# PEER of a two-block network on one core: one-hot in pairs of tokens, a ring of 66 results, and another place for the first reads of the routing weights

## The chip, the cores and the metric

The kernel runs on one core of one Trainium2 chip. The metric is device time in microseconds (us). The engines of a core work in parallel and meet through semaphores: TensorE (PE, with PEld for its weight loads), VectorE (DVE), ScalarE (ACT), GpSimd (POOL) and SyncE (SP), which here only issues transfers. Sixteen DMA engines carry the transfers of all queues.

## What is computed

The reference is a small network over 256 tokens of width 1024, in fp32: a first block (two layers, each SwiGLU, convolution and attention, SwiGLU) and a second block (two layers, each a mixer and a PEER feed-forward). The change touches PEER alone, which runs twice:

```python
def peer_ffn(h, w_query, sub_keys, expert_u, expert_v):      # h: 256 x 1024
    q = (ht @ w_query).reshape(T, 8, 2, 128)
    scores = einsum('thpd,hpkd->thpk', q, sub_keys)          # 128 keys a half
    s_top, i_top = lax.top_k(scores, 16)
    cand = s_top[:, :, 0, :, None] + s_top[:, :, 1, None, :]
    cand_idx = i_top[:, :, 0, :, None] * 128 + i_top[:, :, 1, None, :]
    best, pos = lax.top_k(cand, 16)                          # 16 of 256, 8 heads
    gates = softmax(best)
    ...                                                      # for each token t, k = 1..128
    a = gelu(einsum('tkd,td->tk', expert_u[idx], xb)) * g
    out = einsum('tk,tkd->td', a, expert_v[idx])
```

There are 16384 experts (128 first indices i times 128 second indices j), and a token uses 128 of them.

## The kernel before

**Dense PEER.** The kernel doesn't gather experts. It multiplies all tokens with all experts and sets the unused ones to zero by a dense table of routing weights, 16384 by 256 tokens. A layer of PEER has these stages on the tensor engine:

1. Queries, key scores and, between them, the first up-weights. The vector engine finds the top 16 meanwhile.
2. **The build of the table** (function `g_products`). Tokens come in 16 groups g of 16. For each token, TensorE multiplies two one-hot matrices of fp16: `Ah` (128 slots by 128 values of i, times the weight, in two parts z) and `Bh` (128 slots by 128 values of j). This gives a 128 x 128 table of the token in PSUM, with 32 matmuls a group. Between the groups TensorE takes 1 or 2 up-weight units in turn (the list `DUE`), 24 in all.
3. **The up-only pairs.** The pairs of up-weight units from NTOP + NBUILD = 29 up to NPAIRS - 1 follow.
4. **The v stage.** For n = 0 to 63: two units of down-weights (`peer_v`), and while there are any left, the pair n + NPAIRS of up-weights.

**Units.** A unit is a 128 x 1024 piece of fp32 weights; a chunk of 1 MB holds two, and SyncE loads it into one of NRAW = 3 raw buffers. ScalarE makes the high part w_hi (L1069), then VectorE the low part w_lo (L1502; for some units of the first stage GpSimd, L2079), then TensorE uses both (L583 to L585 for up-weights, L588 to L590 for down-weights). There are NPAIR = 4 buffers of w_hi and w_lo, so w_hi of a unit waits until TensorE has used the unit four places ahead of it. A chunk's load waits for the w_lo of the chunk three places ahead of it.

**Who does what in the build.** VectorE makes the one-hots (`g_onehots`), in order: `Bh` for 16 tokens (L2002), `eqA` (L2005), `Ah` (L2007). Each of `Bh` and `Ah` has two buffers. TensorE waits for them with `oh_ready`. ScalarE empties the four PSUM banks of a group into `stage` (L1421), which has two buffers, and `g_store` (L1407) writes it to the DRAM array `gates`, 1 MB a group. The store of group g - 1 is issued after the first bank of group g is emptied, and that first bank waits until the store of group g - 2 has landed.

**From up to down.** The results of the up-weights, after gelu (L1369), stand in the ring `R` of NRING = 64 tiles of 128 x 256. `products(n)` multiplies two of them by routing weights read back from `gates` (VectorE L2021), then ScalarE (L1435) and VectorE (L2025) split the result in `p_hi` and `p_lo`, and TensorE's down-weight matmuls wait for that. The routing weights are read back in 16 parts of 1 MB into the four buffers `G`; the first four by SyncE (L2124), the others by ScalarE (L1410). `G` lies where `Bh`, `Ah` and `stage` were, so SyncE first waits for every store of the layer (`g_stored`). VectorE makes w_lo of the units up to three ahead of the last up-only unit before it starts `products(0)`; ScalarE puts the gelu of the last up-only pair before its part.

**The order of the work** is written out by hand. `weight_order` gives the order of the chunks, one list for all engines: up-weights up to NPAIRS - 1, then v 0, u NPAIRS, v 1, u NPAIRS + 1 and so on. Every engine runs its own instructions in order; SyncE issues one chunk after the other, and what it waits for holds up all behind it. In the trace tiles of the shared arena read `at`.

Of the kernel before, what the change touches and what calls it, by code (L numbers as in the profile page):

```python
# [10 lines left out]
HF = mybir.dt.float16  # L11
U32 = mybir.dt.uint32
I32 = mybir.dt.int32
ALU = mybir.AluOpType
# [10 lines left out]
NRAW = 3  # L25
NPAIR = 4
NEG = -1e30
NRING = 64
NPOOL = 11
NTURN = 15  # L30
NTOP = 17
# [2 lines left out]
NPAIRS = NRING // 2  # L34
# [63 lines left out]
def carver(place, at=0):  # L98

    state = [at]  # L100

    def take(*shape, dt=FP):
        v = place(state[0], *shape, dt=dt)
        n = int(np.prod(shape))
        state[0] += (n if dt is not HF else (n + 1) // 2) + 7 & ~7
        return v

    return take, state
# [58 lines left out]
def build(nc, a, out):  # L167
    ctx = ExitStack()
    with ctx:
# [14 lines left out]
        iota = sb("iota", [128, 128], HF)  # L184
# [10 lines left out]
        whi = sb("w_hi", [128, NPAIR, UNIT], FR)  # L195
        wlo = sb("w_lo", [128, NPAIR, UNIT], FR)
        qeps = sb("qeps", [128, 2])
        NA = 32000
        arena_at = (nc.sbuf_base + 511) // 512 * 512 + 128
        sb("gap", [128, arena_at - (nc.sbuf_base + 31) // 32 * 32], mybir.dt.uint8)  # L200
        assert (nc.sbuf_base + 31) // 32 * 32 == arena_at
# [25 lines left out]
        order, unit, n_units = weight_order(a)  # L227
# [234 lines left out]
        carve, end = carver(place)  # L462
# [4 lines left out]
        carve, end = carver(place)  # L467
# [12 lines left out]
        carve, end = carver(place, 14336)  # L480
        mdiag = carve(62, 128)
        carve, end = carver(place, -(-end[0] // T) * T)
# [14 lines left out]
        carve, end = carver(place)  # L497
# [35 lines left out]
        jT = carve(T, dt=HF)  # L533
        iT = carve(T, dt=HF)
        gp = carve(2, T, dt=HF)
        carve, end = carver(place)
        Bh = [carve(16, 128, dt=HF) for _ in range(2)]
        eqA = carve(128, 16, dt=HF)
        Ah = [carve(2, 128, 16, dt=HF) for _ in range(2)]
        stage = [carve(128, 16) for _ in range(2)]  # L540
# [38 lines left out]
        def _(e):  # L579
# [363 lines left out]
            def peer(l):  # L943
# [49 lines left out]
                def g_products(g):  # L993
                    j = g % 2
                    w.wait_ge(oh_ready, oh_ready(l, g))
                    for i in range(4):
                        b = take(gb, ("g", l, g, i))
                        for k in range(4):
                            for z in range(2):
                                t = e.matmul(b[:, k * 128:(k + 1) * 128], Ah[j][:, z, :, 4 * i + k], Bh[j][:, 4 * i + k, :], start=z == 0, stop=z == 1)  # L1000
                        t.then_inc(g_done.hit(l, g, i), 1)

                done = 2 * NTOP
# [482 lines left out]
        def _(e):  # L1486
# [407 lines left out]
            def peer(l):  # L1894
# [103 lines left out]
                def g_onehots(g):  # L1998
                    j, t = g % 2, slice(g * 16, g * 16 + 16)
                    if g >= 2:  # L2000
                        w.wait_ge(g_done, g_done(l, g - 2, 3))
                    e.tensor_tensor(Bh[j], jT[:, t].unsqueeze(2).broadcast_to([128, 16, 128]), iota.unsqueeze(1).broadcast_to([128, 16, 128]), ALU.is_equal)  # L2002
                    if g >= 1:
                        w.wait_ge(oh_ready, oh_ready(l, g - 1))
                    step(e.tensor_tensor(eqA, iT[:, t].unsqueeze(1).broadcast_to([128, 128, 16]), iot, ALU.is_equal))  # L2005
                    stepped()
                    e.tensor_tensor(Ah[j], eqA.unsqueeze(1).broadcast_to([128, 2, 128, 16]), gp[:, :, t].unsqueeze(2).broadcast_to([128, 2, 128, 16]),  # L2007
                                    ALU.mult).then_inc(oh_ready.hit(l, g), 1)
# [60 lines left out]
        @block.gpsimd  # L2069
        def _(e):  # L2070
            w = Waits(e)

            def peer(l):
                q, seen = PEER_Q[l], 0
                for k, half, lo, n in halves:
                    if lo == "p" and unit[("peer_q", l), 0] <= n <= unit[("peer_v", l), 127]:
                        w.wait_ge(hi_done, hi_done(n))
                        for c in (slice(0, 512), slice(512, 1024)):
                            t = e.tensor_tensor(wlo[:, n % NPAIR, c], raw(k, half)[:, c], whi[:, n % NPAIR, c].bitcast(FP), ALU.subtract)  # L2079
                        t.then_inc(w_lo_pool.hit(n), 1)  # L2080
                        seen += 1
                        if seen == NPAIR:
                            w.wait_ge(x_upd, x_upd(q, 7))
                            w.wait_ge(iota_set, 1)
                            e.tensor_copy(ioa, iota16.unsqueeze(2).broadcast_to([128, 16, 128]))
                            e.tensor_copy(iot, iota.unsqueeze(2).broadcast_to([128, 128, 16])).then_inc(iot_ready.hit(l), 1)

            w.wait_ge(hook_free, hook_free(0))
            e.dma_start(scratch, brow).then_inc(bias_out.sem, 16)
            w.wait_ge(bias_out, 16)  # L2090
            for hh in range(4):
                e.dma_start(skew[:, hh * 256:(hh + 1) * 256],
                            bass.AP(tensor=scratch.tensor, offset=hh * 384, ap=[[1, 128], [1, 256]])).then_inc(bias_skew.sem, 16)
            for l in range(L):
                w.wait_ge(qk_inv, qk_inv(l))
                e.tensor_copy(mrx[:, 2:4].rearrange("p i t z (m d) -> p (i t z m) d", m=2),
                              mr[:, 2:4].rearrange("p i t z m -> p (i t z m)").unsqueeze(2).broadcast_to([128, 16, 64])).then_inc(qk_wide_p.hit(l), 1)
            w.wait_ge(x_upd, x_upd(5, 7))
            e.dma_start(dm, a["decay"]).then_inc(decay_in.sem, 16)
            e.dma_start(posi, a["positions_2"].partition_broadcast(128)).then_inc(pos_in.sem, 16)  # L2100
            peer(0)
            peer(1)


        @block.sync
        def _(e):
            w = Waits(e)
            for k, (src, lo, n) in enumerate(order):
                if 0 < k < NRAW:
                    w.wait_ge(loads["x"], 16)  # L2110
                elif k >= NRAW:
                    _, before, m = order[k - NRAW]
                    if before == "ada":
                        w.wait_ge(ada_done, ada_done(2 * m + 1))
                    else:
                        w.wait_ge(lo_done[before], lo_key[m + 1][1])
                e.dma_start(raw_t[:, k % NRAW, :], src).then_inc(landed[k % NRAW].sem, 16)
                for l in range(L):
                    if n == unit[("peer_v", l), 0] and lo != "ada":
                        for i in range(2):  # L2120
                            w.wait_ge(g_stored[i], 128 * (l + 1))
                    for c in range(4):
                        if n == unit[("peer_v", l), 2 * c] and lo != "ada":
                            e.dma_start(G[c], gates[l, :, :, c * 128:(c + 1) * 128].rearrange("g p c -> p g c")).then_inc(g_read[c].sem, 16)  # L2124
            for m in range(KT):
                w.wait_ge(fin_ready, fin_ready(m))
                e.dma_start(out[:, m, :], fin[:, m, :]).then_inc(stored.sem, 16)
            w.wait_ge(stored, 16 * KT)
            w.wait_ge(bias_out, 16)
# [123 lines left out]
```

## Time and profile before

| | us |
|---|---|
| median of 3 runs | 3195.18 |
| lowest, highest | 3187.87, 3199.23 |
| the profiled execution | 3191.61 |
| its span in the trace | 3189.8 |

The span lies within 2 us of its own execution's time, so the trace accounts for nearly all of it. The profiled execution is 3.6 us below the median of the three runs, and their spread is 11 us. Times in the trace are counted from the span's start. PEER of the first layer of the second block runs from about 1293 us on, that of the second from about 2364 us. "Layer 0" and "layer 1" below are these two.

In the trace a matmul of 256 columns lasts 0.28 us while the next starts after 0.12 us, since matmuls overlap: the rate is read from the starts. PEclk is TensorE's granted clock as a share of 2.4 GHz.

### The profile page before, as it was taken

The page shows a single profiled execution, that of the slowest core. Times are in us where ns is not written, and L with a number is a line of the kernel's source. Part 1 is how long each engine was busy: PE and PEld are TensorE (multiplying, and loading weights), DVE is VectorE, ACT ScalarE, POOL GpSimd, SP SyncE. Part 2 cuts the span into 40 slices and gives each one's busy share as a digit, 9 for nine tenths or more (in the row PEclk, how much of TensorE's full clock was granted, in tenths as well). Part 3 has the DMA queues.
Part 4 walks back from the last instruction along what each step waited for, and adds up shares of the span by engine and source line. Part 5 has one row for each costly group of instructions (what it writes and reads, how often), then busy time and mean ns, then how long its engine had stood idle before and what let it go on. Part 6 is the DMA issues. An engine that isn't in the chain of part 4 may idle for free.

```text
span 3189.8 us, 53578 instructions
## 1 busy us (share of the span) xinstructions
PE 3073.3 (96%) x22724; PEld 2890.7 (91%) x22724; DVE 2209.0 (69%) x3454; ACT 1622.3 (51%) x2442; POOL 186.9 (6%) x153
## 2 busy tenths in 40 slices
PE   8999999999999999999899999999989999999998
PEld 7998999999899889999899998878989998999887
DVE  5767786776687645799655556766658995555676
ACT  5645554655454445455444444456444554444444
POOL 0000000000000000730000000000037000000000
PEclk9999999999999999999999999999999999999999
DMA  6663476775277444446766566645445567666663
GB/s 221 241 241 112 171 265 242 254 257 185 69 259 265 172 165 153 159 172 244 254 230 219 205 210 236 215 175 187 159 156 187 198 254 254 219 211 213 222 232 125
DMA packets 153262, 654.63 MB, mean 205 GB/s; under 512 B 10332, under 2 KB 77472, under 8 KB 78272
## 3 DMA queue, kind: packets, MB, share of 16 engines
q1 hardware_dynamic: 96576, 584.09, 51.3%
q10 hardware_dynamic: 56032, 65.66, 6.4%
q8 instruction: 180, 2.95, 0.4%
q0 software_dynamic: 416, 1.45, 0.2%
q14 instruction: 58, 0.48, 0.0%
HBM read 616.55 MB, written 34.61 MB: 204 GB/s over the span
## 4 chain that ended last, share of the span: by engine, by line
PE 72%; DVE 19%; ACT 5%; DMA 2%; issue 1%; POOL 1%; ACTq 0%; DVEq 0%; SPq 0%
PE ps L583 14%; PE ps L585 14%; PE ps L584 14%; PE ps L588 8%; PE ps L590 8%; PE ps L589 8%; DVE w_lo L1502 6%; DVE at L2007 2%; DVE at L2002 2%; ACT w_hi L1069 2%; PE ps L739 1%; DVE raw L1497 1%; DVE at L2005 1%; DVE at L1643 1%; POOL w_lo L2079 1%
## 5 line engine op out<-in xcount | busy, mean ns | idle before, releaser
L1502 DVE TENSOR_TENSOR w_lo<-raw,w_hi 128x1024 fp32r<-128x1024 f32 x932 | 1134.7, 1224 | 660.2 <-ACT w_hi L1069 659.2
L1069 ACT ACTIVATE w_hi<-raw 128x1024 fp32r<-128x1024 f32 x1000 | 1051.0, 1055 | 708.3 <-PE ps L585 436.7
L583 PE MATMUL ps<-h_hi,w_hi 128*128 128x256 f32 x4224 | 1191.5, 282 | 22.6 <-DVE w_lo L1502 17.1
L584 PE MATMUL ps<-h_lo,w_hi 128*128 128x256 f32 x4224 | 1179.8, 279 | 0.0
L585 PE MATMUL ps<-h_hi,w_lo 128*128 128x256 f32 x4224 | 1179.7, 279 | 0.0
L583 PEld LDWEIGHTS ps<-h_hi,w_hi 128*128 128x128 f32 x4224 | 798.8, 189 | 31.7 <-issue 17.7
L585 PEld LDWEIGHTS ps<-h_hi,w_lo 128*128 128x128 f32 x4224 | 802.7, 190 | 0.0
L584 PEld LDWEIGHTS ps<-h_lo,w_hi 128*128 128x128 f32 x4224 | 797.2, 189 | 2.9 <-issue 0.2
L588 PE MATMUL ps<-w_hi,at 128*128 128x512 f32 x1024 | 401.4, 392 | 13.6 <-DVE at L2025 13.6
L589 PE MATMUL ps<-w_lo,at 128*128 128x512 f32 x1024 | 400.8, 391 | 0.0
L590 PE MATMUL ps<-w_hi,at 128*128 128x512 f32 x1024 | 400.6, 391 | 0.0
L583 PE MATMUL ps<-at,w_hi 128*128 128x256 f32 x1024 | 291.4, 285 | 3.9 <-DVE at L1811 1.4
L585 PE MATMUL ps<-at,w_lo 128*128 128x256 f32 x1024 | 287.7, 281 | 0.0
L584 PE MATMUL ps<-at,w_hi 128*128 128x256 f32 x1024 | 287.6, 281 | 0.0
L2079 POOL TENSOR_TENSOR w_lo<-raw,w_hi 128x512 fp32r<-128x512 f32 x136 | 173.1, 1307 | 1409.9 <-ACT w_hi L1069 1409.8
L588 PEld LDWEIGHTS ps<-w_hi,at 128*128 128x128 f32 x1024 | 193.7, 189 | 51.5 <-issue 13.9
L590 PEld LDWEIGHTS ps<-w_hi,at 128*128 128x128 f32 x1024 | 193.5, 189 | 40.5
L589 PEld LDWEIGHTS ps<-w_lo,at 128*128 128x128 f32 x1024 | 193.8, 189 | 37.7
L583 PEld LDWEIGHTS ps<-at,w_hi 128*128 128x128 f32 x1024 | 193.3, 189 | 5.0 <-DVE at L1811 1.6
L585 PEld LDWEIGHTS ps<-at,w_lo 128*128 128x128 f32 x1024 | 195.8, 191 | 0.0
L584 PEld LDWEIGHTS ps<-at,w_hi 128*128 128x128 f32 x1024 | 193.8, 189 | 0.0
L1369 ACT ACTIVATE at<-ps 128x512 f32<-128x512 f32 x128 | 76.5, 598 | 196.0 <-PE ps L585 196.0
(274 smaller groups left out, 3138.0 us busy)
## 6 DMA issues: line engine op xcount, KB each, us to landing
raw<-in_peer_u SPq DMA_DIRECT2D x128, 1024.0 KB, 4.8
raw<-in_peer_v SPq DMA_DIRECT2D x128, 1024.0 KB, 4.8
raw<-in_ffn_gu SPq DMA_DIRECT2D x88, 1024.0 KB, 4.9
raw<-in_ada_w SPq DMA_DIRECT2D x48, 1024.0 KB, 5.1
raw<-in_ffn_down SPq DMA_DIRECT2D x44, 1024.0 KB, 4.9
gates<-at ACTq DMA_DIRECT2D x32, 1024.0 KB, 5.4
at<-gates ACTq DMA_DIRECT2D x24, 1024.0 KB, 6.0
raw<-in_w_in SPq DMA_DIRECT2D x16, 1024.0 KB, 4.8
```

The lines of the kernel that those rows point to most:

```text
L583: e.matmul(o, lhs[0], rhs[0], start=start, stop=False)
L584: e.matmul(o, lhs[0], rhs[1], start=False, stop=False)
L585: return e.matmul(o, lhs[1], rhs[0], start=False, stop=stop)
L588: e.matmul(o, lhs[0], rhs[0], start=start, stop=False, skip_group_check=True)
L589: e.matmul(o, lhs[0], rhs[1], start=False, stop=False, skip_group_check=True)
L590: return e.matmul(o, lhs[1], rhs[0], start=False, stop=stop, skip_group_check=True)
L1069: e.activation(whi[:, u % NPAIR, :], raw(k, half), ACT.Copy).then_inc(hi_done.hit(u), 1)
L1369: e.activation(R[:, i:i + 2, :].rearrange("p a b -> p (a b)"), bank["u", l, n], ACT.Gelu_apprx_tanh).then_inc(u_done.hit(l, n), 1)
L1502: e.tensor_tensor(wlo[:, m % NPAIR, :], raw(k, half), whi[:, m % NPAIR, :].bitcast(FP), ALU.subtract).then_inc(w_lo_dve.hit(m), 1)
L2002: e.tensor_tensor(Bh[j], jT[:, t].unsqueeze(2).broadcast_to([128, 16, 128]), iota.unsqueeze(1).broadcast_to([128, 16, 128]), ALU.is_equal)
L2007: e.tensor_tensor(Ah[j], eqA.unsqueeze(1).broadcast_to([128, 2, 128, 16]), gp[:, :, t].unsqueeze(2).broadcast_to([128, 2, 128, 16]), ALU.m ...
L2079: t = e.tensor_tensor(wlo[:, n % NPAIR, c], raw(k, half)[:, c], whi[:, n % NPAIR, c].bitcast(FP), ALU.subtract)
```

## The change

1. `Bh` is laid out as 8 pairs of tokens x 128 values of j x 2 tokens, where it was 16 tokens x 128 values of j. The comparison that writes it (L2002) has the two tokens of a pair innermost: `jT` is read as a pair, repeated 128 times, and in place of `iota` there is `iota2`, in which each value of j stands twice. The matmul reads the column of a token as `Bh[j][:, 2 * i + k // 2, :, k % 2]`, that is 128 values of 2 bytes at a pitch of 4 bytes, where they lay side by side.
2. GpSimd writes `iota2` (128 x 256 fp16) once a layer, between its two other copies of this kind (L2085, L2086).
3. NRING is 66, so NPAIRS is 33: there are four up-only pairs (29 to 32), and the v stage starts one pair later and takes 31 pairs of up-weights along. The arena grows from 32000 to 32512 words.
4. The wait for the stores and the first four reads of the routing weights stand in SyncE's order behind the up-weight chunk that follows v 0, v 1, v 2 and v 3, where they stood behind v 0 to v 3 themselves.

```diff
-NRING = 64
+NRING = 66
...
-        NA = 32000
+        NA = 32512
...
+        iota2 = carve(128, 2, dt=HF)
         carve, end = carver(place)
-        Bh = [carve(16, 128, dt=HF) for _ in range(2)]
+        Bh = [carve(8, 128, 2, dt=HF) for _ in range(2)]
...
-                                t = e.matmul(b[:, k * 128:(k + 1) * 128], Ah[j][:, z, :, 4 * i + k], Bh[j][:, 4 * i + k, :], start=z == 0, stop=z == 1)
+                                t = e.matmul(b[:, k * 128:(k + 1) * 128], Ah[j][:, z, :, 4 * i + k], Bh[j][:, 2 * i + k // 2, :, k % 2], start=z == 0, stop=z == 1)
...
-                    e.tensor_tensor(Bh[j], jT[:, t].unsqueeze(2).broadcast_to([128, 16, 128]), iota.unsqueeze(1).broadcast_to([128, 16, 128]), ALU.is_equal)
+                    e.tensor_tensor(Bh[j], jT[:, t].rearrange("p (a r) -> p a r", r=2).unsqueeze(2).broadcast_to([128, 8, 128, 2]),
+                                    iota2.unsqueeze(1).broadcast_to([128, 8, 128, 2]), ALU.is_equal)
...
                             e.tensor_copy(ioa, iota16.unsqueeze(2).broadcast_to([128, 16, 128]))
+                            e.tensor_copy(iota2, iota.unsqueeze(2).broadcast_to([128, 128, 2]))
                             e.tensor_copy(iot, iota.unsqueeze(2).broadcast_to([128, 128, 16])).then_inc(iot_ready.hit(l), 1)
...
-                    if n == unit[("peer_v", l), 0] and lo != "ada":
+                    if n == unit[("peer_u", l), 2 * NPAIRS] and lo != "ada":
                         for i in range(2):
                             w.wait_ge(g_stored[i], 128 * (l + 1))
                     for c in range(4):
-                        if n == unit[("peer_v", l), 2 * c] and lo != "ada":
+                        if n == unit[("peer_u", l), 2 * (NPAIRS + c)] and lo != "ada":
                             e.dma_start(G[c], gates[l, :, :, c * 128:(c + 1) * 128].rearrange("g p c -> p g c")).then_inc(g_read[c].sem, 16)
```

**SyncE's queue where the v stage's loads begin**, before:

```order
L2117 DMA raw<-in_peer_u 128x2048 [waits w_lo_done_dve] x18
L2117 DMA raw<-in_peer_v 128x2048 [waits w_lo_done_dve]
L2124 DMA at_267_268<-gates 128x16x128 [waits g_stored1,g_stored0]
L2117 DMA raw<-in_peer_u 128x2048 [waits w_lo_done_dve]
L2117 DMA raw<-in_peer_v 128x2048 [waits w_lo_done_dve]
L2124 DMA at_269_270<-gates 128x16x128
L2117 DMA raw<-in_peer_u 128x2048 [waits w_lo_done_dve]
```

and in the changed kernel:

```order
L2120 DMA raw<-in_peer_u 128x2048 [waits w_lo_done_dve] x19
L2120 DMA raw<-in_peer_v 128x2048 [waits w_lo_done_dve]
L2120 DMA raw<-in_peer_u 128x2048 [waits w_lo_done_dve]
L2127 DMA at_269_270<-gates 128x16x128 [waits g_stored1,g_stored0]
L2120 DMA raw<-in_peer_v 128x2048 [waits w_lo_done_dve]
L2120 DMA raw<-in_peer_u 128x2048 [waits w_lo_done_dve]
L2127 DMA at_271_272<-gates 128x16x128
```

The read of the first part of the routing weights, with its wait for the stores, has moved behind one more up-weight chunk, and one more up-weight chunk stands ahead of v 0.

**VectorE at the end of the build and the start of products(0)**, before (the `at` tiles are, by their lines, `Bh`, `eqA`, `Ah`, then the ring and `p_lo`):

```order
L1502 TENSOR_TENSOR w_lo<-raw,w_hi 128x1024 [waits w_hi_done] x2
L2002 TENSOR_TENSOR at_253_254<-at_245_246,iota 128x2048 [waits g_done]
L2005 TENSOR_TENSOR at_255_256<-at_247_248,at_265_266 128x2048 [waits oh_ready]
L2007 TENSOR_TENSOR at_259_260<-at_255_256,at_249_250 128x4096 [waits dve_step]
L1502 TENSOR_TENSOR w_lo<-raw,w_hi 128x1024 [waits w_hi_done] x9
L2021 TENSOR_TENSOR at_225_226<-at_225_226,at_267_268 128x512 [waits g_read0,u_done]
```

and in the changed kernel:

```order
L1503 TENSOR_TENSOR w_lo<-raw,w_hi 128x1024 [waits w_hi_done] x2
L2003 TENSOR_TENSOR at_255_256<-at_245_246,at_251_252 128x2048 [waits g_done]
L2007 TENSOR_TENSOR at_257_258<-at_247_248,at_267_268 128x2048 [waits oh_ready]
L2009 TENSOR_TENSOR at_261_262<-at_257_258,at_249_250 128x4096 [waits dve_step]
L1503 TENSOR_TENSOR w_lo<-raw,w_hi 128x1024 [waits w_hi_done] x11
L2023 TENSOR_TENSOR at_225_226<-at_225_226,at_269_270 128x512 [waits g_read0,u_done]
```

The comparison of `Bh` reads another tile than `iota`, and two more w_lo stand between the last one-hots and `products(0)`.

## Rows read from the trace of the kernel before

**Rows 1.** The page, part 1: busy time, share of the span, instructions.

```profile
PE 3073.3 (96%) x22724; PEld 2890.7 (91%) x22724; DVE 2209.0 (69%) x3454; ACT 1622.3 (51%) x2442; POOL 186.9 (6%) x153
```

**Rows 2.** Chain that ended last, layer 0: start, us, what.

```profile
1538.65 2.27 DVE w_lo L1502 x2
1540.92 2.20 DVE at L2002
1543.13 1.15 DVE at L2005
...
1544.30 2.29 DVE at L2007
...
1548.89 11.04 DMA raw<-in_peer_v
...
1561.06 8.94 DMA raw<-in_peer_u
...
1572.25 0.69 DVE at L2021
...
1572.97 0.42 ACT at L1435
...
1573.42 0.44 DVE at L2025
```

**Rows 3.** Stretches: length, busy PE, PEld, DVE, ACT, POOL; PEclk, DMA share, GB/s.

```profile
1437.79:1548.66 110.87, 102.25 (x1066) 99.82 (x1065) 110.36 (x69) 60.75 (x96) 0.00 (x0) 0.97 0.68 247
2508.91:2620.45 111.54, 102.19 (x1067) 100.03 (x1065) 111.03 (x69) 61.80 (x98) 0.00 (x0) 0.97 0.67 246
1565.26:1573.99 8.73, 0.00 (x0) 0.03 (x1) 2.40 (x4) 2.26 (x4) 0.00 (x0) 0.75 1.09 365
1574.00:1582.00 8.00, 8.00 (x23) 6.37 (x24) 4.00 (x6) 2.73 (x4) 0.00 (x0) 0.63 0.74 275
2637.65:2642.49 4.84, 0.00 (x1) 0.03 (x1) 2.39 (x4) 2.26 (x4) 0.00 (x0) 0.89 1.09 350
```

**Rows 4.** Groups of instructions: shapes, count, busy us, mean ns, idle before.

```profile
L2002 DVE TENSOR_TENSOR at<-at,iota 128x2048 f16<-128x2048 f16 x32 | 73.1, 2285 | 0.0
...
L2005 DVE TENSOR_TENSOR at<-at,at 128x2048 f16<-128x2048 f16 x32 | 39.0, 1219 | 0.0
...
L1369 ACT ACTIVATE at<-ps 128x512 f32<-128x512 f32 x128 | 76.5, 598 | 196.0 <-PE ps L585 196.0
```

**Rows 5.** Line L2002 in layer 1: shortest/median/longest ns, first and last start.

```profile
L2002 DVE TENSOR_TENSOR at<-at,iota x16: 2283/2285/2287, 2500.4 to 2611.4; 128x2048 f16<-128x2048 f16 x16
```

**Rows 6.** PE, instructions in order of time, late in the build of layer 0.

```profile
1523.98 2.79 PE L1000 MATMUL ps<-at,at 128*128 128x128 f16 x32 [1.79 <-DVE at L2007]
...
1529.32 0.28 PE L583 MATMUL ps<-h_hi,w_hi 128*128 128x256 f32 x1
1529.44 0.28 PE L584 MATMUL ps<-h_lo,w_hi 128*128 128x256 f32 x1
```

**Rows 7.** SyncE's queue, layer 0, in order of time.

```profile
1560.63 0.39 SPq L2124 DMA_DIRECT2D at<-gates  x1
1561.06 2.67 SPq L2117 DMA_DIRECT2D raw<-in_peer_u  x1
```

**Rows 8.** DMA issues, layer 0: 13 stores, last store, first read; us to landing.

```profile
gates<-at ACTq DMA_DIRECT2D x13, 1024.0 KB, 5.4
...
gates<-at ACTq DMA_DIRECT2D x1, 1024.0 KB, 9.9
...
at<-gates SPq DMA_DIRECT2D x1, 1024.0 KB, 6.9
```

**Rows 9.** ACT in order of time: the longest wait for a store in layer 0.

```profile
1543.66 0.60 ACT L1421 ACTIVATE at<-ps 128x512 f32<-128x512 f32 x1 [4.87 <-DMA gates<-at]
```

**Rows 10.** POOL's copy by line, and PE's wait behind it in layer 0.

```profile
L2086 POOL COPY at<-iota 128x2048 f16<-128x2048 f16 x2 | 3.8, 1888 | 0.0
...
1309.63 0.36 PE L583 MATMUL ps<-h_hi,w_hi 128*128 128x256 f32 x1 [1.59 <-POOL w_lo L2079]
```

## The prediction

> **What bounds the kernel now.** I read the busy shares first, then the stretches of PEER, then the chain of work that ended last. TensorE is busy for 3073 of 3190 us [rows 1], so nearly all of the kernel goes at its pace, and an edit can gain only where it stands still or runs at a low clock. PEER has two such places in each layer.
>
> The first is the build of the table. Over it VectorE is busy for 110.4 of 110.9 us in layer 0 and 111.0 of 111.5 in layer 1, while TensorE has gaps of 8.6 and 9.4 us and a mean granted clock of 0.97 [rows 3]. The chain runs through VectorE without a break: Bh 2.20 us, eqA 1.15, Ah 2.29, then one or two w_lo of 1.14 [rows 2]. So VectorE sets the end of this stage, and TensorE waits for one-hots.
>
> The second is the change from up-weights to down-weights. TensorE stands still for 8.7 us in layer 0 and 4.8 in layer 1, and then works for some 6 us at the lower of its two clocks, 1.2 GHz: in the 8 us after the stop the mean is 0.63 of 2.4 GHz [rows 3]. The chain shows why [rows 2]: two loads end to end, v 0 (11.0 us) and u 32 (8.9 us). Chunk u 32 was issued at 1561.06, right behind the first read of the routing weights at 1560.63 [rows 7], which had to wait for the last store, 9.9 us from issue to landing [rows 8]. VectorE must make w_lo of u 32 before it starts products(0). The read itself landed after 6.9 us [rows 8], at 1567.5, before u 32 (1570.0). So it is the chunk behind the read that is late, and not the routing weights.
>
> **Part 1: Bh in pairs.** The old comparison takes 2285 ns, eqA, with as many elements and every operand at a step of one innermost, 1219 [rows 4]. In the new one all operands have two elements at a step of one innermost. The bounds are 1219 and 2285. I take 1219, since Ah, with operands in short repeated rows too, goes at that rate: 4096 elements in 2.29 us [rows 2]. In the chain Bh counts 2.20 and eqA 1.15, so a group gets 1.05 us shorter: 5.64 becomes 4.59, and over 32 groups VectorE saves 33.6 us.
>
> TensorE can't use all of that. Its gaps in the build of layer 0 sum to 8.6 us. Each of some ten stops hides 0.16 more, because the last matmul's row is 0.28 long where the next would have started after 0.12 [rows 6]: 1.7 us by that estimate. A clock of 0.97 over 110.9 us costs 3.3. That is 13.6 us, so its own work is 110.9 - 13.6 = 97.3 us. For layer 1 it is 9.4 + 1.7 + 3.3 = 14.4, which leaves 97.1. VectorE needs 16 x 4.59 + 23 w_lo x 1.14 = 99.7 us after the change, but starts earlier. In layer 1 its first Bh starts at 2500.4 [rows 5], the first one-hots are ready at 2505.0, TensorE takes them at 2508.9, and the last are ready at 2600.1 where TensorE wants them at 2508.9 + 97.1 - 2.2 = 2603.8. The lead stays at about 4 us. **TensorE becomes the bound of the build**, and the comparison could be 4 / 16 = 0.25 us slower than I take it before that changes. Full gain 13.6 + 14.4 = 28.0. I take off 2.5 for waits that move in from ScalarE and the stores (rival B): 25.5.
>
> The Trainium skill, Vector Engine (DVE) Microarchitecture Reference, section 5.1, has the two-per-tick mode for two-byte operands if every innermost step is one and every innermost row has more than one element; a row of two meets it, and by that rule the sum stands. Section 5.2 of the same page speaks against it: a port keeps its rate only in runs of at least two adjacent 4-byte words, and a pair of jT is one such word, read over and over. Its table has 1.73 against 1.054 ns for one source that hops at every element; as an estimate from that page this makes 1219 ns into 2.0 us. No row here shows rows of two elements, so it is part of rival A, and the sum would be 3171.
>
> **Part 2: the matmul's operand at a pitch of 4 bytes.** Same count, other reads. The fp32 matmuls move one 4-byte element after the other at 0.12 us for 256 columns [rows 6], 0.45 ns a column, so this pitch is known to run. Bounds: nothing, and half that rate (rival D). I take nothing.
>
> **Part 3: iota2.** GpSimd copies 256 elements more before it goes on with w_lo, and TensorE waits for that w_lo right after the copies, 1.59 us [rows 10], so nothing covers it. A copy of 2048 elements takes 1.89 us [rows 10]: between an eighth, 0.24, and all of it. I take 0.3, near the eighth, a layer: 0.6 lost.
>
> **Part 4: ring of 66, and the read one chunk later.** No work is added: one pair of up-weights moves ahead of the v stage, which then takes one less along. Count from T, TensorE's end of the build. A unit takes 24 x 0.115 = 2.75 us, so the up-only stretch lasts 22 us now (8 units) in place of 16.5 (6). The last store landed when the first read went out, at 1560.6 [rows 7], 9.9 us after its issue [rows 8], so it was issued 2 us after T; I leave both, and it lands at T + 12. The chunk u 33 no longer stands behind it. It needs w_lo of u 31, which needs TensorE to have used u 29: about T + 8. It lands by T + 19 even at the 11 us of v 0 [rows 2]. The read goes out at T + 12 and lands after 6.9 at T + 19. VectorE reaches products(0) only after w_lo of u 33, whose w_hi waits until TensorE has used the first half of u 32, at T + 19: so at T + 21.5. Both transfers are in time, by 0 and 2 us. What is late next is the handover itself: TensorE ends u 32, then gelu 0.6 [rows 4], p_hi 0.42, p_lo 0.44 [rows 2] and some 0.3 between them make **a stop of 1.8 us** in each layer. A lone stop of that length would not, I take it, be followed by the low clock.
> Gain in layer 0: 8.7 + 8 x (1 - 0.63) = 11.7, less 1.8, makes 9.9. In layer 1, with the clock's cost taken as the same: 4.8 + 3.0 - 1.8 = 6.0. Together 15.9. Moved past on SyncE's queue are only the reads 0 to 3, each behind one chunk. Reads 1 to 3 serve products(4), (8) and (12), which are three pairs away or more, and cost nothing.
>
> **The sum.** 25.5 + 15.9 - 0.6 = 40.8 us. Against the profiled execution, 3191.6, this gives 3150.8; the median of the runs shown is 3.6 above that execution, so I forecast 3154.
>
> **Rivals.**
> A. The pair layout doesn't run at two elements a tick: Bh stays at 2285 ns, or, by the run-of-words rule, at 2.0 us. For it: no instruction here has operand rows of two elements. Against it: Ah's short rows. Then the build gains nothing (or 16 x 0.28 = 4.5 us a layer) and only part 4 is left: 3195 - 15.9 + 0.6 = 3180 (or 3171).
> B. The stores set the pace of the build. A store is issued after the first bank of the next group and must land before the first bank of the group after that, so one period less 0.6 us. Now the period is 110.9 / 15, 7.4 us; at TensorE's pace it would be 6.35, which leaves 5.75 against a median of 5.4 [rows 8]. One wait of 4.87 us happens even now [rows 9], and the DMA engines, at a share of 0.68 and 247 GB/s [rows 3], must move the same bytes in 99 us. If the mean landing grows to 6.1 the period is 6.7, the build takes 15 x 6.7 + 2.2 = 103, and each layer gains 4.5 less than forecast: 3163.
> C. The stop stays. The same stores, chunks and the read fall in the 20 us after T, where the DMA share is 1.09 now [rows 3]; margins of 0 and 2 us are thin. If u 33 or the read comes late by as much as u 32 does today, part 4 gives only some 2 us: 3168.
> D. **Slower than before:** the products' moving operand at a pitch of 4 bytes runs at half rate. Then each of the 1024 products takes 128 x 0.45 = 58 ns longer, all of it on TensorE, which sets the pace by then: 59 us, or 3213. It decides from 40.8 us / 1024 = 40 ns a product on. Against it stands the rate of the fp32 matmuls.
>
> **How the numbers follow.** A measurement of this kernel tells about 0.3%, 10 us, from no change. Chances: forecast 0.58, A 0.12 (0.04 of it at 3171), B 0.14, C 0.10, D 0.04, something unseen 0.02. The low end of the range has no loss in the build and no iota2 cost (3151) and runs as far below their median as the lowest of before (7 us), with 2 to spare: 3142. The high end takes in A: 3181. D, the unseen and the edges, about 0.15, are left out. Faster by over 0.3% hold the forecast, B, C and nearly all of A: 0.92. Within it, 0.04, and slower, 0.04.
>
> **What would show it.** Bh at 1.22 us (right) or 2.0 to 2.3 (A). In the build, no wait of TensorE for Ah, a length of 97 to 100 us and a granted clock of 1.00 (right); VectorE with gaps in place of TensorE. More and longer waits of ScalarE for stores, with TensorE waiting in turn: B. At the first down-weight matmul, a wait of 1.5 to 2 us behind p_lo (right) or of 5 to 9 with a load or a read ahead of it in the chain (C). 32 products in 2.2 us (right) or about 4 (D). What would make the forecast wrong besides is a low clock in spite of short stops, some 3 us each time.

## The result

| | median us | lowest to highest | ratio to before (95%) |
|---|---|---|---|
| before, same chip | 3196.10 | 3187.87 to 3199.23 | |
| changed | 3152.39 | 3149.13 to 3160.27 | 0.9875 (0.9859 to 0.9891) |

The changed kernel is 1.25% faster, 43.7 us by the medians. Its profiled execution took 3149.65 us with a span of 3147.8, against 3191.61 and 3189.8: 42.0 us less, where the sum of the prediction had 40.8. So the comparison below is of two executions that differ by nearly what the medians differ by.

The busy shares of the changed kernel (they answer [rows 1]):

```profile
PE 3061.2 (97%) x22724; PEld 2883.0 (92%) x22724; DVE 2174.6 (69%) x3454; ACT 1623.9 (52%) x2442; POOL 187.8 (6%) x155
```

VectorE has 34.4 us less to do, its count unchanged; GpSimd has two instructions more. The two builds and the 8 us after the first down-weight matmul (length, busy PE, PEld, DVE, ACT, POOL; PEclk, DMA share, GB/s):

```profile
1439.98:1538.58 98.60, 98.60 (x1066) 98.04 (x1066) 94.60 (x68) 62.74 (x98) 0.00 (x0) 1.00 0.76 289
2486.90:2585.20 98.30, 98.30 (x1066) 97.75 (x1066) 94.16 (x68) 62.41 (x98) 0.00 (x0) 1.00 0.75 287
1562.00:1570.00 8.00, 8.00 (x46) 7.06 (x47) 5.18 (x7) 3.80 (x5) 0.00 (x0) 1.00 0.86 263
```

Against [rows 3] the builds are 12.3 and 13.2 us shorter, 25.5 together. TensorE has no gap left in them and the full clock, VectorE has gaps. After the stop the granted clock is 1.00 where it was 0.63, and 46 matmuls fall into the 8 us where it was 23.

The groups of instructions (shapes, count, busy us, mean ns, idle before):

```profile
L1001 PE MATMUL ps<-at,at 128*128 128x128 f16 x1024 | 74.0, 230 | 0.0
L1422 ACT ACTIVATE at<-ps 128x512 f32<-128x512 f32 x128 | 67.5, 602 | 31.5 <-PE ps L1001 27.8 <-DMA gates<-at 3.1
...
L2003 DVE TENSOR_TENSOR at<-at,at 128x2048 f16<-128x2048 f16 x32 | 38.9, 1217 | 0.0
L2007 DVE TENSOR_TENSOR at<-at,at 128x2048 f16<-128x2048 f16 x32 | 38.9, 1217 | 0.0
```

The comparison that writes `Bh` (now L2003) takes 1217 ns where it took 2285 [rows 4], just as long as `eqA` (L2007). The products of the build wait for nothing. ScalarE waits 3.1 us in all for stores; before, a single wait was 4.87 [rows 9].

The chain that ended last, at the first down-weight matmul of layer 0 (start, us, what):

```profile
1536.41 2.17 PE ps L1001 x32
...
1560.45 0.60 ACT at L1370
1561.05 0.31 ACT at L1436
1561.38 0.44 DVE at L2027
1561.82 0.14 issue
1561.95 0.47 PE ps L589
```

Where [rows 2] has `Bh`, `eqA`, `Ah` and two loads, there is now TensorE's own work up to 1560.45 and then gelu, p_hi, p_lo. PE in order of time shows the stop that is left, 1.54 us in either layer (8.73 and 4.84 before):

```profile
1561.95 0.47 PE L589 MATMUL ps<-w_hi,at 128*128 128x512 f32 x1 [1.54 <-DVE at L2027]
...
2608.67 0.47 PE L589 MATMUL ps<-w_hi,at 128*128 128x512 f32 x1 [1.54 <-DVE at L2027]
```

**The account.** Builds 25.5. Stops, with the low clock after them: 8.73 - 1.54 and 3.0 of clock in layer 0, 4.84 - 1.54 and 2.9 in layer 1 (a mean of 0.64 there before), 16.4. Waits of TensorE behind GpSimd's w_lo grew by 1.1 in all (5.4 to 6.5). That is 40.8 of the 42.0. It is the same figure as the prediction's sum by chance, since two of its terms differ. The rest, 1.2, I assign to nothing; the last section shows how large such a rest can be.

Behind the wait for GpSimd in layer 0 the clock falls now, which it didn't before (a mean of 1.00 over the 8 us behind that wait):

```profile
1310.20:1318.20 8.00, 8.00 (x55) 8.00 (x56) 7.83 (x31) 1.60 (x3) 8.00 (x7) 0.79 0.36 133
```

In layer 1 it is the other way round, 0.79 before and 1.00 now. Each time it costs some 1.7 us (8 x 0.21), so the two cancel in this sum.

### The profile page after: what moved, and what is told of

Same layout as the page of the kernel before. It is cut to its first block, busy times and chain, and to the rows that moved or that the text cites. A ratio compares the mean times of both kernels' runs of the same rounds, so it can differ in the third digit from the quotient of the medians.

```text
span 3147.8 us, 53578 instructions
## 1 busy us (share of the span) xinstructions
PE 3061.2 (97%) x22724; PEld 2883.0 (92%) x22724; DVE 2174.6 (69%) x3454; ACT 1623.9 (52%) x2442; POOL 187.8 (6%) x155
## 4 chain that ended last, share of the span: by engine, by line
PE 81%; DVE 11%; ACT 5%; POOL 1%; issue 1%; DMA 1%; ACTq 0%; DVEq 0%
PE ps L584 17%; PE ps L586 17%; PE ps L585 17%; PE ps L589 8%; PE ps L590 8%; PE ps L591 8%; DVE w_lo L1503 3%; PE ps L1001 2%; ACT w_hi L1070 2%; PE ps L740 1%; DVE raw L1498 1%; DVE at L1644 1%; POOL w_lo L2081 1%; ACT at L1125 1%; PE ps L649 1%
## 5 line engine op out<-in xcount | busy, mean ns | idle before, releaser
L584 PEld LDWEIGHTS ps<-h_hi,w_hi 128*128 128x128 f32 x4224 | 796.2, 188 | 30.6 <-issue 16.2
```

Of the source, the lines that this page charges most:

```text
L584: e.matmul(o, lhs[0], rhs[0], start=start, stop=False)
```

## The experiments

Theory: VectorE set the pace of the build, and a load behind the first read made the stop; each of the edits does its own share (pairs 25, ring and read 15). Rivals were that the ring or the read alone does the work at the stop, that VectorE still holds the build, and that GpSimd's copies cost more than taken. All diffs are against the changed kernel. Each ratio is to the kernel before on the same chip.

### The pairs alone

```diff
-NRING = 66
+NRING = 64
...
-                    if n == unit[("peer_u", l), 2 * NPAIRS] and lo != "ada":
+                    if n == unit[("peer_v", l), 0] and lo != "ada":
...
-                        if n == unit[("peer_u", l), 2 * (NPAIRS + c)] and lo != "ada":
+                        if n == unit[("peer_v", l), 2 * c] and lo != "ada":
```

> The pair layout alone: Bh in pairs of tokens with iota2 as in the changed kernel, but a ring of 64 and the first reads of the routing weights behind v 0 to v 3, as before. My theory: each part acts in its own place. The builds then get 25.5 us shorter, iota2 costs 0.8, and the stops at the first down-weights stay as they were (8.7 and 4.8 us, each with some 3 us of the low clock): 3196 - 25 = 3171. Rival: the two parts hang together. A shorter build crowds the stores, the last of them lands later after the end of the build, and the stops grow by some 3 us each: 3177. Second rival: a shorter build leaves the stores as they are but the loads get less crowded, and the stops shrink: 3165 or less.

Measured: 3159.44 us (3159.10 to 3160.22), 0.9889 (0.9869 to 0.9909). That is 36 us of the 43, where 25 were expected. The builds are as in the changed kernel (98.2 us), so the surplus lies at the stops. SyncE's queue of this kernel in layer 0, and then PE at the two stops:

```profile
1536.12 0.33 SPq L2120 DMA_DIRECT2D raw<-in_peer_v  x1
1547.70 0.39 SPq L2127 DMA_DIRECT2D at<-gates  x1
1548.14 1.28 SPq L2120 DMA_DIRECT2D raw<-in_peer_u  x1
```

```profile
1560.33 0.48 PE L589 MATMUL ps<-w_hi,at 128*128 128x512 f32 x1 [3.01 <-DVE at L2027]
```

The queue has the order of before, and yet the stops are 3.01 and 3.26 us, not 8.7 and 4.8. The build ends at T = 1540.7 here. The load of v 0 goes out at T - 4.6; before it went out at T + 0.2 (1548.89 in [rows 2], T = 1548.7). The reason stands on VectorE's own line. The last `Ah` and the next w_lo in the pairs-alone kernel, and the same place before (start, us, engine, line):

```profile
1531.35 2.29 DVE L2009 TENSOR_TENSOR at<-at,at 128x4096 f16<-128x4096 f16 x1
1533.56 2.54 DVE L1503 TENSOR_TENSOR w_lo<-raw,w_hi 128x1024 fp32r<-128x1024 f32 x2
```

```profile
1544.30 2.29 DVE L2007 TENSOR_TENSOR at<-at,at 128x4096 f16<-128x4096 f16 x1
1546.51 3.49 DVE L1502 TENSOR_TENSOR w_lo<-raw,w_hi 128x1024 fp32r<-128x1024 f32 x3
```

VectorE now starts the last `Ah` 9.4 us before T; before it was 4.4. The w_lo behind it, and the loads that wait for those, move ahead with it. So v 0 has landed (after 4.8 us, at 1540.93) before the last store goes out at 1541.59 (T + 0.9). The store takes 6.0 us from issue to landing, against 9.9 [rows 8], where v 0 was issued 1.8 us ahead of it and was still on its way. The first read goes out right behind its landing, at 1547.70. The faster comparison paid twice, once in the build and once at the stop 20 us behind it.

The stop that is left is the chunk behind the read, as before. The chain of the pairs-alone kernel:

```profile
1547.08 0.96 ACT w_hi L1070
1548.14 8.20 DMA raw<-in_peer_u
1556.36 1.07 ACT w_hi L1070
```

and a stop of 3 us is still followed by the lower clock: a mean of 0.79 over the 8 us behind it, in both layers, so 1.7 us each time.

```profile
1560.33:1568.33 8.00, 8.00 (x32) 6.61 (x33) 4.00 (x6) 3.39 (x5) 0.00 (x0) 0.79 0.83 298
2612.03:2620.03 8.00, 8.00 (x32) 6.62 (x33) 4.00 (x6) 3.40 (x5) 0.00 (x0) 0.79 0.73 269
```

Stop and clock are 4.7 and 5.0 us here, 1.54 twice in the changed kernel: 6.6 between them, and the medians say 7. From before they fall by 7.0 and 2.7; with the builds (25.8) and the copies' wait (0.7 more), 25.8 + 9.7 - 0.7 = 34.8 of the 36 between the medians. The two profiled executions are only 31.4 us apart: this one comes to the first build 4.7 us later than the kernel before did (1442.46 against 1437.80), in a part that the edit hardly touches. The last section shows where such differences come from.

### The ring and the reads alone

```diff
-        Bh = [carve(8, 128, 2, dt=HF) for _ in range(2)]
+        Bh = [carve(16, 128, dt=HF) for _ in range(2)]
...
-                                t = e.matmul(b[:, k * 128:(k + 1) * 128], Ah[j][:, z, :, 4 * i + k], Bh[j][:, 2 * i + k // 2, :, k % 2], start=z == 0, stop=z == 1)
+                                t = e.matmul(b[:, k * 128:(k + 1) * 128], Ah[j][:, z, :, 4 * i + k], Bh[j][:, 4 * i + k, :], start=z == 0, stop=z == 1)
...
-                    e.tensor_tensor(Bh[j], jT[:, t].rearrange("p (a r) -> p a r", r=2).unsqueeze(2).broadcast_to([128, 8, 128, 2]),
-                                    iota2.unsqueeze(1).broadcast_to([128, 8, 128, 2]), ALU.is_equal)
+                    e.tensor_tensor(Bh[j], jT[:, t].unsqueeze(2).broadcast_to([128, 16, 128]), iota.unsqueeze(1).broadcast_to([128, 16, 128]), ALU.is_equal)
...
-                            e.tensor_copy(iota2, iota.unsqueeze(2).broadcast_to([128, 128, 2]))
```

> The ring of 66 and the later read alone: Bh as before, without iota2. My theory: the builds stay at 111 us each, the stops fall from 8.7 and 4.8 us to 1.5 each and the low clock behind them goes: 16.5 us, so 3196 - 16 = 3180. Rival: most of the gain at the stops came from the shorter build (transfers that were issued earlier against it), so that here stops of some 4 us stay: 3188.

Measured: 3179.82 us (3173.83 to 3186.41), 0.9949 (0.9932 to 0.9966): 15 us gained. The build of layer 0 and TensorE's waits in this kernel:

```profile
1448.60:1559.50 110.90, 101.36 (x1067) 98.75 (x1065) 110.39 (x69) 61.90 (x98) 0.00 (x0) 0.98 0.68 248
```

```profile
PE ps L1001 <- DVE at L2008: 20.5, 17, 1.8
```

VectorE fills the build as before, TensorE waits for `Ah` 17 times (the line's columns: us in total, times, longest), and the stops are 1.5 us. Here the last store, issued at 1560.37, takes what the prediction had taken:

```profile
gates<-at ACTq DMA_DIRECT2D x1, 1024.0 KB, 10.3
```

```profile
1559.70 0.33 SPq L2118 DMA_DIRECT2D raw<-in_peer_u  x1
...
1570.71 0.39 SPq L2125 DMA_DIRECT2D at<-gates  x1
```

A load was issued 0.7 us ahead of it and is still on its way until 1568.80. What is issued behind the store matters less: v 0 follows 2.7 us behind it here, and just so in the changed kernel, where the store takes 6.0. All 26 last stores of the traces kept divide in this way. The six that take 7.9 to 11.2 us have a load issued 0.7 to 2.3 us ahead of them that lands 4.7 us or more after they are issued; ahead of the other twenty, which take 5.2 to 6.2, the load had landed or landed within 1 us. No run changed this alone.

With T = 1559.5 the read goes out at T + 11.2, and still the stop is only the handover. So part 4 works in the surroundings for which the prediction worked it out. The two parts by themselves gain 36 and 15, together 43: some 8 us are counted by both, and they are the share of the stop that the pairs remove already.

### Pairs with one of the two others

The reads at their old place, with the ring of 66:

```diff
-                    if n == unit[("peer_u", l), 2 * NPAIRS] and lo != "ada":
+                    if n == unit[("peer_v", l), 0] and lo != "ada":
...
-                        if n == unit[("peer_u", l), 2 * (NPAIRS + c)] and lo != "ada":
+                        if n == unit[("peer_v", l), 2 * c] and lo != "ada":
```

> The changed kernel with the first four reads of the routing weights, and the wait for the stores, back behind v 0 to v 3; pairs and ring of 66 stay. My theory: chunk u 33 is then issued behind the read at 12 us after the end of the build, takes about 9, and w_hi, w_lo and the products follow: the first down-weight matmul at T + 25 in place of T + 23.5. Stops of about 3.5 us in place of 1.5, perhaps with a low clock of some 2 us: 3152 + 4 = 3156, at most 3160. Rival: the ring of 66 did it all, and the place of the read is worth nothing: 3152, stops of 1.5 us.

Measured: 3155.88 us (3150.11 to 3159.63), 0.9875 (0.9852 to 0.9899). The time lies where it was expected, but the stops are 1.54 us each, the rival's value, and its ratio is that of the changed kernel. SyncE's queue of this kernel:

```profile
1545.70 0.33 SPq L2120 DMA_DIRECT2D raw<-in_peer_v  x1
1549.09 0.39 SPq L2127 DMA_DIRECT2D at<-gates  x1
1550.70 1.16 SPq L2120 DMA_DIRECT2D raw<-in_peer_u  x1
```

The chunk behind the read goes out 1.6 us after it. It is not the read that holds it, which is issued by 1549.48, but the w_lo that frees its raw buffer; VectorE ends that one at 1550.67. The last store has landed before, at 1549.01, so the read's place costs nothing.

A ring of 64 with the reads at their new place:

```diff
-NRING = 66
+NRING = 64
```

> The changed kernel with a ring of 64; pairs and the later read stay. My theory: the up-only stretch is 16.5 us again, the read goes out about 12 us after the end of the build and lands at T + 19, so products(0) waits for the read itself: first down-weight matmul at T + 20.8, stops of about 4.3 us with the low clock of some 3 us behind them: 3152 + 2 x 5.5 = 3163. Rival: the place of the read did it all, and the extra pair covers nothing: 3152, stops of 1.5 us.

Measured: 3153.69 us (3149.13 to 3155.12), 0.9873 (0.9853 to 0.9893), where 3163 was expected. PE at the stop, and the queue:

```profile
1556.47 0.47 PE L589 MATMUL ps<-w_hi,at 128*128 128x512 f32 x1 [1.54 <-DVE at L2027]
```

```profile
1541.92 0.33 SPq L2120 DMA_DIRECT2D raw<-in_peer_u  x1
1545.33 0.39 SPq L2127 DMA_DIRECT2D at<-gates  x1
```

u 32 goes out ahead of the read, 3.4 us after T, and the read itself waits only for the store. 16.5 us of up-only work are enough for both.

So with the pairs in place **one of the two edits is enough**, and neither is 7 us worse. What the second one adds is below what these runs can tell.

### How far VectorE is from the build's end

```diff
-                    e.tensor_tensor(Bh[j], jT[:, t].rearrange("p (a r) -> p a r", r=2).unsqueeze(2).broadcast_to([128, 8, 128, 2]),
+                    if g < 2:
+                      e.tensor_tensor(Bh[j], jT[:, t].rearrange("p (a r) -> p a r", r=2).unsqueeze(2).broadcast_to([128, 8, 128, 2]),
                                     iota2.unsqueeze(1).broadcast_to([128, 8, 128, 2]), ALU.is_equal)
```

> The changed kernel, but Bh is written only for groups 0 and 1 of each layer; the other fourteen groups multiply with what stands in the buffers. This leaves out part of the computation (the one-hots of the second index), and takes 14 x 1.15 = 16 us a layer off VectorE and nothing off TensorE. My theory: TensorE is the bound of the build now, so the build stays at 98 to 99 us and the whole at 3152. Rival: VectorE, ScalarE and TensorE still hold each other up, and a lighter VectorE brings more: 3152 - 2 x 3 = 3146 or less.

This kernel leaves out 14 of the 16 comparisons for `Bh` in each layer, so its result is not PEER's; only its time counts. Measured: 3154.88 us (3151.01 to 3157.97), 0.9876 (0.9853 to 0.9899). The build of layer 0:

```profile
1442.46:1540.82 98.36, 98.36 (x1067) 97.81 (x1065) 78.53 (x55) 59.11 (x95) 0.00 (x0) 1.00 0.76 276
```

VectorE has 16.2 us less to do, and the build lasts 98.4 us, where it lasts 98.5 between the same two matmuls of the changed kernel. TensorE is the bound of the build; a still cheaper `Bh` would bring nothing.

This kernel also meets the timetable that the prediction feared. A load is issued 2.1 us ahead of the last store of layer 0. The store goes out at T + 2.2 (T = 1540.8) and lands at T + 12.3, where the read goes out too, and the read lands at T + 20.4. The stop is 1.54 us even so, in both layers. With the ring of 66 and the later read together, a late store costs nothing.

### GpSimd's copies later

In the first stage of PEER GpSimd makes the w_lo of some units. Its copies, three with `iota2`, stand behind the fourth of these, and TensorE waits for the w_lo behind them. In the changed kernel (PE in order of time):

```profile
1310.20 0.36 PE L584 MATMUL ps<-h_hi,w_hi 128*128 128x256 f32 x1 [2.35 <-POOL w_lo L2081]
```

The wait was 1.59 [rows 10]. Two kernels move the copies behind its 16th and 28th unit:

```diff
-                        if seen == NPAIR:
+                        if seen == 4 * NPAIR:
```

> The changed kernel, but GpSimd makes its three copies (ioa, iota2, iot) after the 16th unit of its w_lo in a layer and not after the 4th. My theory: at the 4th unit nothing is made ahead, the 4.3 us of copies lie on the path, and TensorE waits 2.3 us for GpSimd right behind them; at the 16th GpSimd is some units ahead and the four buffers cover the copies: 2 x 2.3 = 4.6 us less, 3148. Rival: GpSimd needs about as long for a unit as TensorE and never gets ahead, so the wait only moves: 3152. Second rival: the end of this stage hangs on VectorE's search for the top 16, whatever TensorE waits for: 3152.

Measured: 3147.81 us (3145.02 to 3151.24), 0.9854 (0.9832 to 0.9877).

```diff
-                        if seen == NPAIR:
+                        if seen == 7 * NPAIR:
```

> As the run with the copies after the 16th unit, but after the 28th of 34. My theory: a later place is as well covered or better, while iot is still ready before VectorE asks for it at the end of the search for the top 16: 3148 or a little less. Rival: it is too late, and VectorE waits for iot, or TensorE waits as before because GpSimd is never ahead: 3152 or above.

Measured: 3151.20 us (3148.05 to 3152.96), 0.9862 (0.9840 to 0.9885). Beside them on that chip the changed kernel itself:

> The changed kernel once more, unaltered, so that the next three runs have it beside them on the same chip. Both theories: 3152, with single runs from 3149 to 3160.

Measured: 3153.49 us (3150.11 to 3158.37), 0.9866 (0.9851 to 0.9881). And unit 16 once more, beside it:

> The changed kernel with GpSimd's three copies after the 16th unit, a second time. My theory: the waits behind the copies (2.3 us a layer) are on the path, so it is 4 to 5 us below the changed kernel beside it: 3148. Rival: the earlier difference of 4.6 us was the spread of the runs: 3152.

Measured: 3147.56 us (3145.35 to 3150.98), 0.9854 (0.9838 to 0.9869). TensorE's waits for w_lo of GpSimd in the unaltered kernel and then in this one (us in total, times, longest):

```profile
PE ps L584 <- POOL w_lo L2081: 6.1, 4, 2.3
```

```profile
PE ps L584 <- POOL w_lo L2081: 1.8, 2, 1.0
```

The waits explain 4.3 of the 5.9 us between the medians. The rest may be the clock: in the unaltered kernel's trace it falls behind both layers' waits for the copies (a mean of 0.79 over 8 us), in the other those waits are gone, and between PEER's start and the build it falls once, behind a wait for VectorE at 2461.85. The two ratios' intervals overlap, and so do the runs, by one each (3145.35 to 3150.98 against 3150.11 to 3158.37), so it is the traces that carry this gain. Units 16 and 28 have the same waits, and the 3.4 us between them lie within the spread of the runs.

### The first products before the last up-only pair

What is left of the stop is a handover: the last up-weight matmul, gelu, p_hi, p_lo, the first down-weight matmul. `products(0)` needs only the results of pair 0. Here ScalarE and VectorE do it ahead of their part in the last up-only pair (NPAIRS - 1):

```diff
-                for n in range(NTOP + NBUILD, NPAIRS):
+                for n in range(NTOP + NBUILD, NPAIRS - 1):
...
+                u_pair(NPAIRS - 1)
...
-                for n in range(NTOP + NBUILD, NPAIRS):
+                for n in range(NTOP + NBUILD, NPAIRS - 1):
...
+                pair(("peer_u", l), NPAIRS - 1)
```

> The changed kernel, but ScalarE and VectorE do products(0) before the last up-only pair (u 32) and not after it. My theory: the stop of 1.5 us a layer is the handover of gelu, p_hi and p_lo alone, and the first read has landed by then, so p_lo(0) is ready long before TensorE is done with u 32: both stops go, 3 us less, 3149. Rival: the read lands at T + 17 and holds ScalarE and VectorE up while they should make w_hi and w_lo, and a stop as long or longer appears elsewhere: 3152 to 3158. With the ring of 64 there would be no time for this; here the extra pair would get a use.

Measured: 3149.50 us (3143.88 to 3161.63), 0.9865 (0.9846 to 0.9885): at the expected place, but with a spread that tells little by itself. The wait is gone from the trace. Then both, this and the copies at unit 16:

> The changed kernel with the copies after the 16th unit and with products(0) before the last up-only pair. My theory: the two gains lie in other stages and add: 3152 - 4.6 - 3 = 3144.5. Rival: at least one of them is none, 3148 or 3152.

Measured: 3144.98 us (3140.16 to 3148.13), 0.9841 (0.9827 to 0.9855). PE where the up-weights end, in this kernel, and its waits behind GpSimd:

```profile
1559.19 0.28 PE L586 MATMUL ps<-h_hi,w_lo 128*128 128x256 f32 x1
1559.30 0.39 PE L589 MATMUL ps<-w_hi,at 128*128 128x512 f32 x1
```

```profile
PE ps L584 <- POOL w_lo L2083: 1.8, 2, 1.0
```

The first down-weight matmul follows 0.11 us after the last up-weight matmul. This version is 49 us below the kernel before on its own chip. By the ratios to that kernel it is 0.25% below the changed one (0.9841 against 0.9866). The intervals of these ratios meet (0.9827 to 0.9855, 0.9851 to 0.9881), but its slowest run, 3148.13, is below the fastest of the changed kernel beside it, 3150.11. The traces show which waits went, 4.3 us and twice 1.54.

## Why the prediction was right, point by point

- **What bounds the kernel.** Right. The pairs alone took VectorE off the chain of the build, and the chunk behind the read was the late one at the stop: with the old order and the ring of 64 it still is, at 3 us.
- **Part 1, `Bh` at 1219 ns.** Right, 1217. By the two-per-tick rule of the Trainium skill (Vector Engine (DVE) Microarchitecture Reference, section 5.1) a row of two elements is enough, and the trace agrees. The 2.0 us that I had worked out from section 5.2 of that page did not come: a word of two elements read over and over costs no more than `eqA`'s rows.
- **Part 1, TensorE becomes the bound.** Right. Its own work was taken as 97.3 and 97.1 us; the builds are 98.6 and 98.3. VectorE's lead of 4 us is 4.9 at the last group: the last `Ah` is ready at 1531.5, TensorE takes it at 1536.41. The term, 25.5, is the measured one, but by luck. 2.5 us were taken off for waits that move in, and TensorE has none there; its own work was 1.3 and 1.2 longer than the gaps and the clock of before made it, which comes to as much.
- **Part 2, the pitch of 4 bytes.** Right, at nothing: 230 ns a product against 232, and 32 of them in 2.17 us.
- **Part 3, iota2.** Somewhat under-sized. The copy takes 0.40 us where 0.3 a layer was taken: with an eighth of the elements it takes more than an eighth of the time (1.89). Over both layers the waits grew by 1.1 here, 0.76 of it behind the copies of layer 0. In the six other traces with the copies at this place they grew by 0.3 to 1.1, in four of them by 0.7. The prediction gave these waits no low clock. The clock did fall behind 10 of the 16 waits of 1.9 to 2.4 us for the copies in the traces with the early copies, the kernel before among them; where it falls it costs more than the growth of the wait.
- **Part 4, the timetable.** The end was right and the way there wrong in one step: "I leave both, and it lands at T + 12". Count from T = 1538.6. SyncE's queue in the changed kernel:

```profile
1541.96 0.33 SPq L2120 DMA_DIRECT2D raw<-in_peer_v  x1
1546.96 0.33 SPq L2120 DMA_DIRECT2D raw<-in_peer_u  x1
1547.41 0.39 SPq L2127 DMA_DIRECT2D at<-gates  x1
```

  The last store went out at 1539.25 and landed 6.0 us later, at T + 6.7. u 33 went out at T + 8.4, as predicted (T + 8), and the read behind it at T + 8.8, not T + 12. u 33 landed after 5.0 us, at T + 13.4, and the read after 8.1, at T + 16.9. Against the T + 19 and T + 21.5 at which they are needed that is room of some 5 us each, where the prediction had 0 and 2, so rival C, the stop that stays, was further off than it seemed. The step kept the store's time of before while part 1 had just moved the load that was on its way when the store was issued. The pairs-alone kernel shows this, at 6.0 us, and the kernel with the old comparison shows the other, at 10.3. The margins of 0 and 2 would have been enough too: with `Bh` for two groups the store lands at T + 12.3, and the stop is 1.54.
- **The handover stop.** 1.54 for 1.8. No low clock follows it, as was taken, in any of the 18 stops of this length in nine traces; behind those of 3 us it does, both times.
- **Whose gain it is.** The sum gave the ring and the reads 15.9 us. That is what they gain alone (15), but on top of the pairs it is only 7, and either edit would do. The sum was right all the same, because it asked what is left at the end, a handover in each layer, and that is the same whichever edit removes the rest. Its split between the parts was wrong.
- **The sum.** 40.8 predicted against 42.0 between the profiled executions, and 3154 against a median of 3152.4. A difference this small is luck in part: the runs of this kernel lie 11 us apart.

## What to carry to other kernels

When an engine is sped up, follow what it releases: here the w_lo behind the one-hots came 5 us earlier, with them a load, and a store at the end of the stage, no longer issued while that load was on its way, took 4 us less, so a second edit had half its work done. The time of a transfer here depended on what was still on its way when it was issued, and a timetable worked out on the old trace needs them worked out again. Once TensorE is at 97%, look for handovers of 1 to 2 us in which the next stage's first input could have been made earlier, and for helpers' work that stands in front of what TensorE needs next; by the traces they were worth 3.1 and 4.3 us here.

## What the runs showed of the hardware beyond that

The same matmul of 256 columns comes at two spacings, both at a granted clock of 1.00. Two runs of 16 in the changed kernel, the first and last of each in order of time:

```profile
1404.80 0.28 PE L584 MATMUL ps<-h_hi,w_hi 128*128 128x256 f32 x1
...
1406.56 0.28 PE L584 MATMUL ps<-h_hi,w_hi 128*128 128x256 f32 x1
```

```profile
1558.44 0.28 PE L586 MATMUL ps<-h_hi,w_lo 128*128 128x256 f32 x1
...
1560.14 0.28 PE L586 MATMUL ps<-h_hi,w_lo 128*128 128x256 f32 x1
```

Fifteen steps take 1.76 us in the one and 1.70 in the other. Over longer stretches they are 117.8 and 113.4 ns, 3.9% apart. A spacing can hold for tens of us and more. In the changed kernel it is 113.4 ns up to 1306, 117.8 from 1314.6, behind the 2.35 us wait and the low clock that follows it, to 1418.7, and 113.4 behind a wait of 1.0 us at 1420. In the second trace of the same kernel (the one run beside the late copies) it goes over to 113.4 where the clock comes back up after the wait for the copies, without a gap in the matmuls. Over a stretch of 100 us the two levels are 3.7 us apart, as much as an edit of this kind.

The two traces of the changed kernel show what this does to a run. Their spans are 3147.8 and 3156.6 us, 8.8 apart. The same 2250 matmuls, far ahead of PEER, take 259.4 us in the one (from 356.6 on) and 267.1 in the other (from 359.1 on), with waits of 1.9 us in both: 7.6 of the 8.8. It is not the chip, since the late copies' trace from the second one's chip has 259.5. A part of that stretch in either trace, with TensorE never idle and at a clock of 1.00:

```profile
555.00:615.00 60.00, 60.00 (x532) 60.00 (x531) 46.97 (x68) 37.08 (x73) 0.00 (x0) 1.00 0.72 259
```

```profile
566.00:626.00 60.00, 60.00 (x512) 60.00 (x511) 47.30 (x68) 40.04 (x79) 0.00 (x0) 1.00 0.69 246
```

532 matmuls start in the 60 us of the one and 512 in those of the other. So most of the difference between two executions of one kernel lay in the spacing, in a part that the change doesn't touch, and a comparison by stages is worth more than one of whole times. The same may be behind the 1.2 us that the account leaves over. What picks the spacing stays open.
